# Fifteen products of a k-step, bank by bank or in three rounds over the five banks

## What is computed

```
z = rmsnorm(h) @ w_in                      # [640, 2048] @ [2048, 6144]
u, gp, q, k, v, gr = split(z)
mix = [pool(u) * silu(gp), groupnorm(retention(rotary(q), rotary(k), v)) * silu(gr)]
h = h + mix @ w_out                        # [640, 2048] @ [2048, 2048]
h = h + sigmoid(rmsnorm(h) @ w_pg) * (p @ w_ple)   # @ [2048, 2048]
```

## Time and profile before

| | |
|---|---|
| median of 3 runs | 2483.32 us |
| the profiled execution's own time | 2485.69 us |
| its span, first to last instruction | 2483.9 us |
| PE busy | 2458.3 us (99%), 11202 matmuls |
| PE weight loads busy | 2006.9 us (81%) |
| DVE / ACT / POOL busy | 1019.7 (41%) / 627.8 (25%) / 201.1 us (8%) |
| mean granted TensorE clock | 0.996 |
| DMA | 259.85 MB, mean 105 GB/s |

### The profile page before, as it was taken

How to read it: one execution, slowest core, us unless ns; L and a number is a source line. 1 busy time by engine, 2 the same in 40 slices (tenths; PEclk the granted TensorE clock), 3 DMA queues, 4 the chain that set the end, 5 groups by cost and what they waited for, 6 DMA issues and landing times.

```text
span 2483.9 us, 27162 instructions
## 1 busy us (share of the span) xinstructions
PE 2458.3 (99%) x11202; PEld 2006.9 (81%) x11202; DVE 1019.7 (41%) x1565; ACT 627.8 (25%) x987; POOL 201.1 (8%) x301
## 2 busy tenths in 40 slices
PE   8999999999999999999999999999999999999997
PEld 6888888888887888888888788788788788888886
DVE  5343343343345234444543423433434542344444
ACT  5121121121132223322332112112122232232223
POOL 1101001001001000000010110110110100000000
PEclk9999999999999999999999999999999999999998
DMA  6343243243244333223242432432432433322322
GB/s 207 98 126 117 72 120 117 78 119 117 79 120 120 98 98 106 77 78 110 82 150 70 132 108 76 132 106 76 133 107 71 132 121 112 106 71 82 94 70 100
DMA packets 175611, 259.85 MB, mean 105 GB/s; under 512 B 15968, under 2 KB 121760, under 8 KB 174208
## 3 DMA queue, kind: packets, MB, share of 16 engines
q1 hardware_dynamic: 143616, 173.38, 22.9%
q0 software_dynamic: 21456, 71.76, 8.7%
q10 hardware_dynamic: 10416, 12.97, 2.2%
HBM read 221.30 MB, written 36.76 MB: 104 GB/s over the span
## 4 chain that ended last, share of the span: by engine, by line
PE 98%; DMA 1%; DVE 1%; ACT 0%; issue 0%; POOL 0%; DVEq 0%; ACTq 0%; SPq 0%; POOLq 0%
PE acc L1262 87%; PE side L1262 8%; PE osb L1457 1%; DMA raw<-in_w_in 1%; PE side L1319 0%; PE side L1420 0%; PE side L1334 0%; DMA Z<-in_x_t 0%; PE side L1364 0%; DVE HT L1247 0%; PE osb L1262 0%; DVE HT L1232 0%; DVE Z L1164 0%; DVE Wlo L784 0%; DVE stage L869 0%
## 5 line engine op out<-in xcount | busy, mean ns | idle before, releaser
L1262 PE MATMUL acc<-Ahi,Whi 128*128 128x512 f32 x2048 | 815.6, 398 | 10.5 <-DVE Wlo L784 10.1
L1262 PE MATMUL acc<-Alo,Whi 128*128 128x512 f32 x2048 | 799.1, 390 | 0.0
L1262 PE MATMUL acc<-Ahi,Wlo 128*128 128x512 f32 x2048 | 798.7, 390 | 0.0
L449 ACT ACTIVATE Whi<-raw 128x1024 fp32r<-128x1024 f32 x320 | 338.9, 1059 | 1504.7 <-PE acc L1262 1492.2
L784 DVE TENSOR_TENSOR Wlo<-raw,Whi 128x1024 fp32r<-128x1024 f32 x320 | 392.2, 1226 | 776.9 <-ACT Whi L449 776.9
L1262 PEld LDWEIGHTS acc<-Ahi,Whi 128*128 128x128 f32 x2048 | 385.1, 188 | 97.1 <-DVE Wlo L784 10.5
L1262 PE MATMUL acc<-Whi,Ahi 128*128 128x512 f32 x1152 | 455.5, 395 | 0.6 <-ACT stage L516 0.5
L1262 PEld LDWEIGHTS acc<-Alo,Whi 128*128 128x128 f32 x2048 | 385.0, 188 | 82.1
L1262 PE MATMUL acc<-Whi,Alo 128*128 128x512 f32 x1152 | 448.6, 389 | 0.0
L1262 PE MATMUL acc<-Wlo,Ahi 128*128 128x512 f32 x1152 | 448.4, 389 | 0.0
L1262 PEld LDWEIGHTS acc<-Ahi,Wlo 128*128 128x128 f32 x2048 | 385.4, 188 | 77.7 <-issue 1.0
(11 more groups left out here) (177 smaller groups left out, 1376.1 us busy)
## 6 DMA issues: line engine op xcount, KB each, us to landing
raw<-in_w_in SPq DMA_DIRECT2D x384, 256.0 KB, 3.0
raw<-in_w_out SPq DMA_DIRECT2D x128, 256.0 KB, 3.3
raw<-in_w_pg SPq DMA_DIRECT2D x128, 256.0 KB, 3.2
Ss<-in_state_ret POOLq DMA_DIRECT2D x64, 256.0 KB, 5.6
out_new_ret_sample<-Ss POOLq DMA_DIRECT2D x64, 256.0 KB, 2.9
X<-kv_parts ACTq DMA_DIRECT2D x16, 384.0 KB, 5.5
kv_parts<-stage ACTq DMA_DIRECT2D x16, 256.0 KB, 2.3
Z<-in_x_t POOLq DMA_DIRECT2D x4, 1024.0 KB, 5.7
```

What stands on the lines that cost most here:

```text
L449: nc.scalar.activation(Whi[:, p % 2], raw[:, p % 2], ACT.Copy).then_inc(w_hi, 1)
L1262: return nc.tensor.matmul(out, lhsT, rhs, start=start, stop=stop)
```

## The change

Steps 0 to 13 no longer take the three products of a bank together. A new `step(s)` goes three times over the five banks: first high x high for banks 0 to 4, then high activations x low weights for the five, then low activations x high weights for the five. The waits of a bank (`inputs`) stand before its first product, in the first round. The last two steps keep the order of before. Operands, number of products, weight loads, and all other engines' programs are the same.

```diff
--- before.py
+++ after.py
@@ -1265,9 +1265,17 @@
 
                 ks, flipped = order_of(q), KINDS[q % G_LAYER] != "kv"
 
-                def tile(s, t):
+                def product(s, t, part, first, last):
+
                     k = ks[s]
                     p, kk = divmod(s, 2)
+                    w = (Whi, Wlo, Whi)[part][:, p % 2, kk]
+                    x = (Ahi, Ahi, Alo)[part][:, k]
+                    if flipped and t < NPT:
+                        return mm(acc[:, t], w[:, t * P:(t + 1) * P], x[:, 0:NP], first, last)
+                    return mm(acc[:, t], x[:, t * P:(t + 1) * P], w, first, last)
+
+                def inputs(s, t):
                     if s == 0 and q:
                         e, n = EMPTIED[q - 1, t]
                         pe.wait_ge(acc_out[e], n)
@@ -1275,18 +1283,23 @@
                         pe.wait_ge(a_lo, (first_of[0] * 3 + first_of[1]) * KT + s + 1)
                     if first_of and first_of != (0, 0) and t == NPT and s % 4 == 0:
                         pe.wait_ge(side_free, freed("s", *first_of, s // 4))
-                    hi, lo = Whi[:, p % 2, kk], Wlo[:, p % 2, kk]
+
+                def step(s):
+
+                    for part in range(3):
+                        for t in range(NT):
+                            if part == 0:
+                                inputs(s, t)
+                            done = product(s, t, part, s == 0 and part == 0, False)
+                    if s % 2:
+                        done.then_inc(w_used, 1)
+
+                def tile(s, t):
+                    kk = s % 2
+                    inputs(s, t)
                     first, last = s == 0, s == KT - 1
-                    if flipped and t < NPT:
-                        cols = slice(t * P, (t + 1) * P)
-                        mm(acc[:, t], hi[:, cols], Ahi[:, k, 0:NP], first, False)
-                        mm(acc[:, t], lo[:, cols], Ahi[:, k, 0:NP], False, False)
-                        done = mm(acc[:, t], hi[:, cols], Alo[:, k, 0:NP], False, last)
-                    else:
-                        tok = slice(t * P, (t + 1) * P)
-                        mm(acc[:, t], Ahi[:, k, tok], hi, first, False)
-                        mm(acc[:, t], Ahi[:, k, tok], lo, False, False)
-                        done = mm(acc[:, t], Alo[:, k, tok], hi, False, last)
+                    for part in range(3):
+                        done = product(s, t, part, first and part == 0, last and part == 2)
                     if kk == 1 and t == NT - 1:
                         done.then_inc(w_used, 1)
                     elif last:
@@ -1295,8 +1308,7 @@
                 for s in range(KT - 2):
                     if s % 2 == 0:
                         pe.wait_ge(w_lo, q * PAIRS + (s // 2 + 3))
-                    for t in range(NT):
-                        tile(s, t)
+                    step(s)
                     jobs(s)
                 pe.wait_ge(w_lo, q * PAIRS + PAIRS + 2)
                 tile(KT - 2, 0)
```

## The result

The changed kernel takes 2510.32 us, median of 4 runs (2508.04 to 2510.56), against 2484.04 us for the kernel before (4 runs, 2482.88 to 2485.19): ratio 1.0103, 95% interval 1.009 to 1.0115. It is 26.3 us slower. Forecast were 22.6 us and 2505.9 us, with a range to 2511. The profiled execution took 2510.21 us (span 2508.4), 24.5 us more than that of before.

A forecast was written before the change was run, and what follows sets the result against it. TensorE, 98% of the chain, was taken to bound the kernel; bank 4's earlier waits at 39 boundaries add 22.6 us, products 0: 2483.3 + 22.6 = 2505.9 us, range 2500 to 2511 us (2499.3 to 2511 with free short waits).

The forecast's parts named there:

- The products: Inside steps, 5600 neighbouring products no longer share a bank: taken as 0, bounds -5.6 to +5.6 us.
- rival of quicker products: Rotation removes a penalty for writing a bank just written; at 8 ns per neighbour 2461 us; 3%.
- an order that doesn't reach the engine: Rival: instructions are still issued bank by bank as before, 2483 us; 1%.
- The price of a wait: In step 0, the product after the one waiting for bank 4 starts 0.39 us after bank 4's read ends.
- E - S: At stream ends: end of bank 4's read minus start of the stream's last product; forecast unchanged, 1.12 to 3.6 us.
- formula E - S - 0.97: Delay in us at each of 39 stream boundaries in the new order, where above zero.
- 30 short boundaries: Uq-to-kv, kv-to-gt, out-to-out, out-to-pg and pg-to-pg stream changes: 0.15 to 0.40 us each, 6.4 us in all.
- The sum: Added waits for bank 4 over 39 boundaries: 3.3 + 0.7 + 2.4 + 10.8 + 3.6 + 1.8 = 22.6 us.
- Short waits free: Rival: weight loads catch up, so short boundaries cost nothing: 16.2 us in all, 2499.5 us; 5%.
- The clock: Rival: TensorE's clock halves for 10 us behind each of nine stalls, 5 us more each, 2551 us; 5%.
- nine long stalls: Waits for bank 4 at six gt-to-uq, two gt-to-out and one pg-to-uq boundaries, 1.9 to 2.6 us each.
- Catching up of VectorE and ScalarE: During the new stalls both run on, so later work gets earlier: taken as no gain, -3 us at most.

The follow-up runs named there:

- Run 1: Changed kernel with step 0 of each stream bank by bank as before, steps 1 to 13 in rounds: 2484.98 us, ratio 1.0000 to the kernel before.
- Run 2: Changed kernel with rounds in step 0 only, steps 1 to 13 bank by bank: 2507.84 us, ratio 1.0094 to the kernel before.
- run 5: Changed kernel with step 0's rounds going over banks 4, 0, 1, 2, 3: 2554.6 us, ratio 1.0283 to the kernel before.
- run 6: Changed kernel with ScalarE reading bank 4 after its first SiLU at each gt stream's end, not the fourth: 2501.2 us, ratio 1.0067 to the kernel before.

## Why the prediction was right, and where it was short

**The products.** Taken at 0 within 5.6 us either way. Run 1 measured 0 within about 2 us. The rival of quicker products (3%) falls with it. That of an order that doesn't reach the engine (1%) falls with the timelines after, where the four `acc<-Ahi,Whi` stand together (129.71, x4).

**The price of a wait.** In both profiles of the changed kernel E - S is within 0.05 us of before at all 39 boundaries, and the formula E - S - 0.97 gives the loss to within 0.1 us at all but the three with a fall of the clock. What is lost over all of step 0 is better given by E - S - 0.95, since the distances behind a stall are some ns longer for a few products. That is 0.02 us at each of the 30 short boundaries, 0.6 us in all; the prediction had it among its bounds (up to 2 us) and not in its sum.

**The sum.** Forecast 22.6 us. Run 2, in whose profile the clock did not fall, gave 23.3 us by the boundaries and 22.9 us by the times. The changed kernel without its clock falls: 28.8 - 2.9 - 2.7 = 23.2 us in the first profile, 27.7 - 1.6 - 2.7 = 23.4 in the second. The row of one boundary did not stand quite for all of its kind. The third gt-to-uq of each layer has E - S = 2.67 to 2.72 in place of 2.88, but there the kernel before lost nothing, so its net is 1.74 to 1.81 all the same. The first pg-to-pg of each layer has 1.23 in place of 1.37, which makes the sum 0.3 us too high.

**Short waits free** (rival, 5%): refuted by runs 2 and 5, in which the shortest waits (E - S = 1.12) cost 0.17 to 0.21 and 1.12 us each.

**The clock** (rival, 5%) is the step that failed in part. The prediction took it as all or nothing, a fall behind all nine long stalls of 10 us each, and left it out of the sum. It came behind two of them in one profile and one in the other, for 3.4 us, at 1.45 to 1.6 us each: 1.6 to 2.9 us. "The mean granted clock is 0.996 all the same", the argument against it, came from waits of at most 0.9 us and said nothing about stalls of 2.6. The Trainium skill (TensorE: Matmul & The Clock Gate, HAM oscillation) warns of idle gaps that halve the clock for the next burst. These rows agree with it in kind, though its gaps are longer than the stalls here: 2.6 us were enough at three of nine. The term should have stood in the sum with a price for each stall that may have it, from 0 to the loss of one short stretch at half clock. With it and the 0.6 us of the short waits the sum gives 22.6 + 0.6 + 1.6 to 2.9 = 24.8 to 26.1 us, beside 24.2 and 26.3 us measured. This is worked out with the runs known, and the tail alone, whose half clock comes earlier or later, moves a single execution by about as much as the difference: the second profile's last stream ended 2.1 us before the first's (2479.43 against 2481.52), but its tail took 29.1 us in place of 26.9.

**Catching up of VectorE and ScalarE** (bound -3 us): none. E - S stayed within 0.05 us. That both engines' work at the end of a stream hangs on TensorE's products of the same stream fits this, and was argued, not tested; at the first gt-to-uq of before, VectorE waited for a side product until 192.38, 8.8 us ahead of S, and from there its work runs on through the group norm to the reads of the banks.

## What to carry to other kernels

In this kernel the order of accumulating products over several banks matters only where the banks change hands: count for each bank how many products stand between the end of its old contents' reading and the first product that needs it, and give the bank that is completed last the largest distance. No product behind a waiting one was taken ahead of it (at gt-to-uq the second round, with bank 0 long free, began at 204.87, behind bank 4's product at 204.54), so a round over all banks makes the first product of the latest bank a barrier for everything behind it. In the other steps both orders cost the same (run 1). If rounds are wanted for another reason, keep step 0 bank by bank.

## What the runs showed of the hardware that was not expected

- Stalls can halve the clock for a short stretch behind them, and not each time. Over the profiles of the changed kernel (two) and run 2: none of 18 stalls of 1.7 to 2.0 us brought it, 3 of 9 stalls of 2.6 us did (and not the one of run 6); in run 5 it was 8 of 9 stalls, which lost 2.7 to 3.6 us before the clock's part. A stretch was 3.4 us at 0.50 (once 6.8) and cost 1.4 to 1.6 us (2.8).
- The clock's fall in the tail came earlier or later against the same code from profile to profile, worth 1.6 us there (3.55 against 1.93 us for the same 16 products) and 1.8 to 2.5 us over the whole tail (28.7 to 29.4 against 26.9 us).
- Whether a product accumulates in the bank of the one ahead of it or in another makes no difference: 0.2267 us both ways.
